# The final norm of one block and the first norm of the next, joined and applied late

## The reference

```
def _rmsnorm(x, w):
    y = xf * lax.rsqrt(jnp.mean(xf * xf, axis=-1, keepdims=True) + EPS)
    return (y * w)
...
hx = hx + 0.5 * mx[:, 8] * fx          # end of the first block's last FFN
return _rmsnorm(hx, final_norm_w)      # replaces the residual
...
h = _rmsnorm_2(x, ffn_pre_norm[0])     # first norm of the second block
x = x + 0.5 * _swiglu_2(h, w_gate, w_up, w_down)
```

## Time and profile before

| | |
|---|---|
| time, median of 3 runs | 2900.47 us (2898.59 to 2901.76) |
| profiled execution, first to last instruction | 2896.7 us |
| PE busy | 2798.4 us (97%) |
| VectorE busy | 1784.3 us (62%) |
| ScalarE busy | 1215.5 us (42%) |
| GpSimd busy | 203.1 us (7%) |
| DMA, mean | 146 GB/s |

### The profile page before, as it was taken

How to read it: one execution, slowest core, us unless ns; L and a number is a source line. 1 busy time by engine, 2 the same in 40 slices (tenths; PEclk the granted TensorE clock), 3 DMA queues, 4 the chain that set the end, 5 groups by cost and what they waited for, 6 DMA issues and landing times.

```text
span 2896.7 us, 45886 instructions
## 1 busy us (share of the span) xinstructions
PE 2798.4 (97%) x17432; PEld 2459.5 (85%) x17432; DVE 1784.3 (62%) x2696; ACT 1215.5 (42%) x1817; POOL 203.1 (7%) x247
## 2 busy tenths in 40 slices
PE   6999999999999999999998999999989999999998
PEld 3888877678888788888876998999879999998998
DVE  6977344847884287632548655556666666657664
ACT  3333223733222243222326554554446555434553
POOL 0100011010100100001010001001000000000001
PEclk9999999999999999999999999999999999999999
DMA  6666332025664346533321555566436656653564
GB/s 264 210 195 191 101 93 87 1 73 167 209 190 115 113 157 196 159 100 98 113 85 37 167 179 159 160 177 208 124 89 181 176 186 184 180 157 96 173 178 127
DMA packets 119326, 424.29 MB, mean 146 GB/s; under 512 B 13408, under 2 KB 14449, under 8 KB 119073
## 3 DMA queue, kind: packets, MB, share of 16 engines
q1 hardware_dynamic: 98640, 351.32, 39.9%
q0 software_dynamic: 19520, 70.19, 8.1%
q10 hardware_dynamic: 1040, 1.05, 0.1%
HBM read 421.45 MB, written 1.05 MB: 146 GB/s over the span
## 4 chain that ended last, share of the span: by engine, by line
PE 89%; DVE 7%; ACT 2%; issue 1%; DMA 1%; SPq 1%; DVEq 0%; ACTq 0%
PE bank L717 28%; PE bank L719 28%; PE bank L718 28%; DVE WL L1539 1%; DVE rstd L1724 1%; DVE g_max L1826 1%; DVE d_small L1888 1%; DMA f_nat<-in_ada_n 1%; PE bank L849 1%; ACT WH L1215 1%; PE bank L953 0%; DVE tn L1734 0%; PE bank L930 0%; DVE g_p L1846 0%; DVE d_p L1897 0%
## 5 line engine op out<-in xcount | busy, mean ns | idle before, releaser
L717 PE MATMUL bank<-XH,WH 128*128 128x256 f32 (+1 forms) x3776 | 1227.5, 325 | 38.3 <-DVE XL L1743 18.0
L1539 DVE TENSOR_TENSOR WL<-raw,WH 128x1024 fp32r<-128x1024 f32 (+1 forms) x664 | 808.2, 1218 | 672.1 <-ACT WH L1215 668.6
L719 PE MATMUL bank<-XH,WL 128*128 128x256 f32 (+1 forms) x3776 | 1215.9, 322 | 0.0
L718 PE MATMUL bank<-XL,WH 128*128 128x256 f32 (+1 forms) x3776 | 1215.9, 322 | 0.0
L1215 ACT ACTIVATE WH<-raw 128x1024 fp32r<-128x1024 f32 (+1 forms) x664 | 682.8, 1034 | 860.2 <-PE bank L719 858.0
L717 PEld LDWEIGHTS bank<-XH,WH 128*128 128x128 f32 x3776 | 723.8, 192 | 100.6 <-issue 28.2
L718 PEld LDWEIGHTS bank<-XL,WH 128*128 128x128 f32 x3776 | 723.9, 192 | 55.1 <-issue 2.9
L719 PEld LDWEIGHTS bank<-XH,WL 128*128 128x128 f32 x3776 | 723.5, 192 | 52.8
L719 PE MATMUL bank<-HH,WL 128*128 128x256 f32 (+1 forms) x1408 | 459.3, 326 | 0.0
L718 PE MATMUL bank<-HL,WH 128*128 128x256 f32 (+1 forms) x1408 | 457.1, 325 | 0.0
L717 PE MATMUL bank<-HH,WH 128*128 128x256 f32 (+1 forms) x1408 | 453.7, 322 | 0.0
(11 more groups left out here) (308 smaller groups left out, 1638.3 us busy)
## 6 DMA issues: line engine op xcount, KB each, us to landing
a_rows<-in_ada_t POOLq DMA_DIRECT2D x124, 512.0 KB, 4.2
raw<-in_ffn_w_gate SPq DMA_DIRECT2D x88, 512.0 KB, 3.7
raw<-in_ffn_w_up SPq DMA_DIRECT2D x88, 512.0 KB, 4.3
raw<-in_ffn_w_down SPq DMA_DIRECT2D x64, 512.0 KB, 3.7
raw<-in_ffn_pre_w_gate SPq DMA_DIRECT2D x44, 512.0 KB, 3.7
raw<-in_ffn_pre_w_up SPq DMA_DIRECT2D x44, 512.0 KB, 4.2
raw<-in_ffn_post_w_gate SPq DMA_DIRECT2D x44, 512.0 KB, 3.6
raw<-in_ffn_post_w_up SPq DMA_DIRECT2D x44, 512.0 KB, 4.2
```

Of the source, the lines that this page charges most:

```text
L717: nc.tensor.matmul(o, WH[:, j % 4, k, :], high, start=start, stop=False)
L718: nc.tensor.matmul(o, WH[:, j % 4, k, :], low, start=False, stop=False)
L719: return nc.tensor.matmul(o, WL[:, j % 4, k, :], high, start=False, stop=stop)
L1539: nc.vector.tensor_tensor(WL[:, b, 0:d, :], raw[:, b, 0:d, :], WH[:, b, 0:d, :].bitcast(F32), ALU.subtract).then_inc(split_done, 1)
```

## The change

The replacing final norm is taken out of the list of steps, and the norm "pre2" of layer 0 becomes `paired_norm`: a late norm with weight w p (`pair_w[:, 0]`). ScalarE squares each residual tile twice, once plainly and once with the scale sqrt(w^2 + eps) (`pair_w[:, 1]`), side by side in `sq`, and GpSimd and TensorE add and sum both at once, 512 wide. Two roots follow; the one with eps^2 goes where a late norm's rstd lies, the other beside it in `rstd[:, S:2S]`. In the down product of the second block's first FFN `restate` turns the residual x into y = x w / sqrt(m(x^2) + eps), one tile at a time, before the tile's update; at tile 0 it takes the reciprocal first. The weights of the pair are made at the start (VectorE) and in the norm with index 1 (ScalarE, a root of 8 columns). The up and down products of this FFN are now read out with rstd multiplied in, as after the other late norms.

```diff
+        eps2 = sb("eps2", [P, 1])
+        pair_w = sb("pair_w", [P, 2, DT])
...
+        def paired_norm():
+            n = norm(S, lambda k, half: pair_w[:, 0, k:k + 1])
+            n["pair"] = True
+            return n
...
-        plain_norm("final_norm_w", 0, "replace")
         for l in range(2):
-            n = plain_norm("pre2", l)
+            n = plain_norm("pre2", l) if l else paired_norm()
...
             def gather_squares(n):
-                t = n["t"]
+                t = 2 * S if n["pair"] else n["t"]
...
             def gathered_sum(n):
+                t = 2 * S if n["pair"] else n["t"]
                 pe.wait_ge(sq_sum, DT * n["i"] + DT - 1)
-                nc.tensor.matmul(bank[6][:, 0:n["t"]], ones_d[:, :], sq[:, 0, 0:n["t"]], start=True, stop=False)
+                nc.tensor.matmul(bank[6][:, 0:t], ones_d[:, :], sq[:, 0, 0:t], start=True, stop=False)
...
             def square(n, k):
+                if n["pair"]:
+                    nc.scalar.activation(sq[:, min(k, 1), S:2 * S], xT[:, k, 0:S], ACTF.Square, scale=pair_w[:, 1, k:k + 1])
                 nc.scalar.activation(sq[:, min(k, 1), 0:t], xT[:, k, 0:t], ACTF.Square).then_inc(sq_ready, 1)
...
             def norm_act(n):
                 act.wait_ge(sq_sum, DT * n["i"] + DT)
+                if n["pair"]:
+                    nc.scalar.activation(rstd[:, 0:S], bank[6][:, S:2 * S], ACTF.Sqrt, bias=eps2[:, 0:1])
+                    nc.scalar.activation(rstd[:, S:2 * S], bank[6][:, 0:S], ACTF.Sqrt, bias=eps[:, 0:1]).then_inc(n_root, 1)
+                    return
                 nc.scalar.activation(rstd[:, 0:t], bank[6][:, 0:t], ACTF.Sqrt, bias=eps[:, 0:1]).then_inc(n_root, 1)
+                if n["i"] == 1:
+                    act.wait_ge(pair_ready, 1)
+                    link(nc.scalar.activation(pair_w[:, 1, :], pair_w[:, 1, :], ACTF.Sqrt))
...
+            def pair_weights():
+                f0, p0 = COL_AT["final_norm_w"], COL_AT["pre2"]
+                w = cols[:, f0:f0 + DT]
+                nc.vector.tensor_tensor(pair_w[:, 0, :], w, cols[:, p0:p0 + DT], ALU.mult)
+                link(nc.vector.tensor_tensor(pair_w[:, 1, :], w, w, ALU.mult))
+                nc.vector.tensor_scalar(pair_w[:, 1, :], pair_w[:, 1, :], EPS, None, ALU.add).then_inc(pair_ready, 1)
...
                     if g.kind == "res" and (b % 3 == 2 or not g.down):
+                        d = res_tile(g, i, b)
+                        if g.scale and g.scale["pair"]:
+                            restate(d)
                         dve.wait_ge(piece_done, q + (j + 1))
-                        d = res_tile(g, i, b)
...
+            def restate(d):
+                if d == 0:
+                    link(nc.vector.reciprocal(rstd[:, S:2 * S], rstd[:, S:2 * S]))
+                w0 = COL_AT["final_norm_w"]
+                link(nc.vector.scalar_tensor_tensor(out=xT[:, d, 0:S], in0=xT[:, d, 0:S], scalar=cols[:, w0 + d:w0 + d + 1],
+                                                    in1=rstd[:, S:2 * S], op0=ALU.mult, op1=ALU.mult))
```

More of the change, by code:

```diff
@@ L262, in build @@
         n_low = sem("n_low")
+        pair_ready = sem("pair_ready")
         sg_ready = sem("sg_ready")
@@ L309, in norm @@
             n["mul0"] = state["mul"]
+            n["pair"] = False
             state["norms"] += 1
@@ L761, in gathered_sum @@
             def gathered_sum(n):
+                t = 2 * S if n["pair"] else n["t"]
                 pe.wait_ge(sq_sum, DT * n["i"] + DT - 1)
-                nc.tensor.matmul(bank[6][:, 0:n["t"]], ones_d[:, :], sq[:, 0, 0:n["t"]], start=True, stop=False)
+                nc.tensor.matmul(bank[6][:, 0:t], ones_d[:, :], sq[:, 0, 0:t], start=True, stop=False)
                 pe.wait_ge(sq_ready, DT * n["i"] + DT)
-                nc.tensor.matmul(bank[6][:, 0:n["t"]], ones_d[:, :], sq[:, 1, 0:n["t"]],
+                nc.tensor.matmul(bank[6][:, 0:t], ones_d[:, :], sq[:, 1, 0:t],
                                  start=False, stop=True).then_inc(sq_sum, 1)
@@ L1527, in _ @@
             nc.vector.memset(ones_1[:, :], 1.0)
+            nc.vector.memset(eps2[:, :], EPS * EPS)
             nc.vector.memset(eps[:, :], EPS).then_inc(hid_low, 2)
@@ L1622, in derive @@
                                                          1.0 if n == 1 else 0.5, None, ALU.mult))
+            def pair_weights():
[4 more added lines that the diff above has]
+                nc.vector.tensor_scalar(pair_w[:, 1, :], pair_w[:, 1, :], EPS, None, ALU.add).then_inc(pair_ready, 1)
             dve.wait_ge(in_loaded, 48)
             release()
+            pair_weights()
             def body(g, i, after):
```

## The result

| | before | after |
|---|---|---|
| median | 2901.11 us (2898.59 to 2901.83, 4 runs) | 2866.68 us (2864.01 to 2870.79, 4 runs) |
| span of the profiled execution | 2896.7 us | 2862.1 us |
| ratio, 95% interval | | 0.9888 [0.9874, 0.9901] |

The change makes the kernel 34.4 us faster. Forecast was 17.9 us, and 2866.7 lies outside the range of 2879 to 2887: the direction was right, the size wrong by a factor of nearly two.

What follows compares the result with a forecast made beforehand. TensorE, busy 97% of the span, was taken as the bound. The seam stage falls from 209.73 to 190.08 + 1.72 = 191.80 us, gaining 17.9, additions elsewhere free: span 2878.8, plus 3.8 gives 2882.5 us, range 2879 to 2887.

Steps and rivals of the forecast that it cites:

- 0.120 us each: Matmul spacing in a 256-column FFN, read from the late stage's 1548 matmuls in 185.75 us; gave 190.08 us for 1584.
- What it adds elsewhere I cost at nothing on the path: Added work outside the seam stage, in down products, evictions, roots and start, was taken as covered: 0 us.
- the term itself: From one down product's end to the next's across the block seam: 209.73 us becomes 191.80, a gain of 17.9.
- The wide sums: TensorE's two sums of squares in the next up product, now 512 wide: 1.72 us, bounds 0.86 and 1.92.
- a later stage that has become longer: Named sign that the forecast was wrong: any later stage taking longer than before.
- The roots: Two Sqrt instead of one in the joined norm: some 0.5 us more, covered by VectorE's 1.33 us wait.
- The restating and its reciprocal: VectorE in the second block's first down product: 0.25 to 0.5 us late, 2.3 at most at tile 0, covered.
- (a): Rival: two late things add up to a 2.6 us TensorE stall at a seam; gain 15.3, 2885.2 us; chance 0.08.
- (b): Rival: norm only joined, not applied late, leaving a 7.6 us gap; gain about 11, 2889.5 us; chance 0.03.
- (c): Rival: weight preparation bounds the two down products, costing from 3.7 us a tile; 6 slower, 2906.5 us; chance 0.04.
- GpSimd's wide additions: Six 512-wide additions in the first down product delay VectorE's weight split by 0.5 us, upper bound 1.82; covered.
- 3.7 us of slack per tile: In the down products, a weight part ready at 2355.00 is used at 2358.70, so lateness up to 3.7 costs nothing.

Runs made afterwards that it cites:

- e1: Kernel before plus an unused 96-byte tile, putting HH and HL where the changed kernel has them (distance 64): 2882.54 us, ratio 0.9945.
- e2: Changed kernel plus an unused 160-byte tile, putting HH back at the old distance of 96 bytes behind the weights: 2885.83 us, ratio 0.9946.
- e11: Changed kernel without restate, so the second block's residual goes on from x: 2868.20 us, ratio 0.9884.
- e7: Changed kernel plus five VectorE multiplications behind restate in each of 8 tiles of the second block's first down product: 2881.98 us, ratio 0.9936.
- e8: Changed kernel plus ten VectorE multiplications behind restate in each of 8 tiles of the second block's first down product: 2904.47 us, ratio 1.0016.
- e6: Changed kernel with 64 unused bytes ahead of XH, so all large tiles move and every distance stays: 2868.54 us, ratio 0.9892.
- e9: Separate kernel of matmul streams alone, 192 each, at set offsets of weights and moving tiles, some with other engines or loads busy: span 853.3 us.
- e12: e10 with all weight buffers alike: distance 0 modulo 256 until the first block's second mixer, weights 64 lower from there: 2853.23 us, ratio 0.9839.
- e5: Changed kernel with 64 unused bytes ahead of raw and the weights, giving XH and HH distance 64 and 0-byte HH offset: 2874.08 us, ratio 0.9903.
- e10: Changed kernel with weight buffers placed by width, 64 past a multiple of 128 for 256 columns, on one for 512: 2834.71 us, ratio 0.9775.
- e3: Kernel before plus an unused 32-byte tile, HH at distance 0 from the weights modulo 128: 2899.57 us, ratio 0.9997.
- e4: Kernel before plus an unused 64-byte tile, HH at distance 32 from the weights modulo 128: 2896.21 us, ratio 0.9984.

## Why the prediction was wrong

**The step that failed** is "0.120 us each", and with it "1584 x 0.120 = 190.08". It was read from a true row, and I took it for a property of the shape and the clock. It depends on the place too. From 1789.17 to 1977.42 the changed kernel takes 188.25 us, not 191.80: 1056 x 0.1200 for the up product, 528 x 0.1133 for the down product and 1.72 for the sums give 188.3. And four other FFNs, which the prediction left out of the sum because no instruction in them is edited ("What it adds elsewhere I cost at nothing on the path"), gave 3.5 us each. 5 x 3.5 = 17.5 us, which e1 gives without the change (16.3 by its span) and e2 takes back. None of the rivals had it, and the range, built from the sums of squares and the spread of the runs, had no term for it. The diff shows the cause in its first two lines, the two new tiles.

**What held.** The seam has no gap, and e2, at the old place, shows the term itself: 18.0 us against 17.9. The wide sums cost 1.72 as said. The clock is 1.00 in the stage, where the earlier trace rows had 0.62 for 4.55 us. The prediction named a later stage that has become longer as a sign of being wrong; the mixer of layer 0 has, by 4.7 us, and what is known of it stands below. The roots: VectorE waits 0.96 for TensorE after the reciprocal (1.33 in the earlier trace rows), so nothing is exposed:

```profile
1796.25 1.75 DVE L1763 RECIPROCAL rstd<-rstd 128x256 f32<-128x256 f32 x1 [2.68 <-ACT rstd L1351]
1798.97 0.42 DVE L1663 TENSOR_TENSOR sg<-bank,rstd 128x256 f32<-128x256 f32 x1 [0.96 <-PE bank L728]
```

The restating and its reciprocal are hidden (e11). The small products at the start take 0.5 us in front of a load that VectorE then waits 2.93 us for (2.31 in the earlier trace rows). Rivals (a), (b) and (c) did not occur.

**GpSimd's wide additions** take 1.30 us each, less than the 1.5 I took. They run beside VectorE's splits, timelines of POOL and DVE:

```profile
1761.27 1.30 POOL L684 TENSOR_TENSOR sq<-sq 128x512 f32<-128x512 f32 x1 [6.18 <-ACT sq L1311]
1768.75 1.30 POOL L684 TENSOR_TENSOR sq<-sq 128x512 f32<-128x512 f32 x1 [6.18 <-ACT sq L1311]
```

```profile
1739.73 2.38 DVE L1559 TENSOR_TENSOR WL<-raw,WH 128x1024 fp32r<-128x1024 f32 x2 [1.17 <-ACT WH L1225]
1762.18 1.47 DVE L1559 TENSOR_TENSOR WL<-raw,WH 128x1024 fp32r<-128x1024 f32 x1 [1.18 <-ACT WH L1225]
1769.65 2.61 DVE L1559 TENSOR_TENSOR WL<-raw,WH 128x1024 fp32r<-128x1024 f32 x2 [1.17 <-ACT WH L1225]
```

The pair at 1739.73 meets no addition and takes 2.38. The pair at 1769.65 begins 0.40 before an addition ends and takes 2.61, and a single split that begins 0.39 before one ends takes 1.47, where one that meets none takes 1.23 (at 1730.67). So about 0.24 us is lost each time (0.28 in the worst of the six), where I took 0.5, on an engine with spare time. The Trainium skill states a full block ("SBUF — State Buffer", section "Who interferes with whom"). Here the loss is less than the overlap, 0.24 of 0.40 us, and with spans on GpSimd being rough the trace neither shows nor refutes it; TensorE waited for no weight part in the whole stretch.

**Right by luck: the slack.** "3.7 us of slack per tile" was read as the time by which one weight part is ready ahead of its use. That is a stock, which is used up once and not renewed: what renews is 7.48 - 6.44 = 1.04 us a tile. The 0.25 to 0.5 us of lateness a tile fitted into either, but rival (c) was priced by the wrong one. It was said to cost from 3.7 us a tile on; e7, with 2.6 us a tile in eight tiles, costs 15.3 us. By the period e7 should add 8 x (2.6 - 1.04) = 12.5 and e8 8 x (5.2 - 1.04) = 33.3; measured were 15.3 and 37.8. The down product itself is 12.2 us longer in e7 (1917.93 to 1989.96 against 59.85 us). Behind it comes a piece that the period doesn't hold: the granted clock is 0.77 in the next 7.44 us, where after had 1.00. In e8 it is 0.91 in the down product itself.

**What stays open.** Why the distance matters at all. For 256 columns, what chooses between 0.1133 and 0.1178 at distance 64: the first was seen alone in the down products of e1, after, e6 and e11, the second alone in e9 without other engines and for nearly all of e12, both at the same addresses in e5, e7, e8 and e10. So the difference between e10 and e12 may be one of this state and not of their places, and e10's time was seen in five runs of one kernel only. The mixers' clock: between the reciprocals around the mixer of layer 0 the kernel before took 164.87 us in its profile, but e1, e3 and e4, the same kernel with a tile that isn't used, took 168.64, 171.05 and 169.87, and the changed one 169.58. So the 4.7 us given back there are no effect of the change that I can show, but perhaps a short value in the one profile of before (e2, with the change, has 171.45); the medians, which hold several executions, are the better measure.

## What to carry to other kernels

A new small tile moves all tiles behind it, and with them the speed of untouched matmuls: work out each large tile's start before and after a change, and compare two versions at equal distances between moving operand and weights, or a change of 18 us looks like one of 34. Then use it: try the distances, since an unused tile is the cheapest experiment there is, and measure matmuls from start to start, or count them in equal windows at full clock, because busy time can't show their spacing. And the slack of a pipelined loop is the period of the bound engine less the helper's work and its own waits in that period, not the time by which one item is ready ahead.

## What the runs showed of the hardware

- Matmuls of 128 x 128 with 256 columns in the rounded form, at the full clock, with TensorE alone follow each other at 0.1200 us when the moving operand begins 0 or 96 bytes behind the weights modulo 128, and at 0.1178 at 32 or 64 (e9). In the kernel the down products have 0.1200 at 96 (before, e2), 0.1187 at 0 (e3), 0.1173 at 32 (e4) and 0.1133 at 64 (e1, after).
- At distance 64 two spacings occur at the same addresses, 0.1133 and 0.1178: by FFN in e5, by tile in e7. In e9 0.1133 came with ScalarE and VectorE busy and stayed after both had stopped.
- With 512 columns the distance counts modulo 256 and the order is another: 0.2267 at 0, 0.2289 at 64, 0.2333 at 32, 96 and 192 (e9); 0.2267 at 0 and 0.2333 at 192 in the kernel's down products (e12 and the changed one). Moving the weights by 64 bytes cost the first block 24 us (e5).
- XH, XL, the weights, HH and HL all moved by the same 64 bytes give 2868.54 against 2866.68 us (e6): no absolute place was seen to count.
- Placing alone gave 32 us of 2867 in one arrangement (e10) and 13 in another (e12).
